# Turning the feed-forward's token-major up tiles by DMA instead of on TensorE, in a two-layer transformer block

## The chip, the cores and the metric

One Trainium2 chip, one NeuronCore of it. The metric is the device time of one execution in microseconds, as the median of several executions. The profile and the trace are of one further execution of the same program.

## The reference, cut to what matters

Two layers, each a mixer of three attention branches followed by a feed-forward block with a short causal convolution. All tensors are fp32: 256 tokens, width 1024, feed-forward width 2816. The change touches the feed-forward only.

```python
def _conv_glu_ffn(x, w_up, conv_w, conv_b, w_down):
    u = x @ w_up                                  # [256, 1024] @ [1024, 5632]
    gate, val = u[..., :D_FF], u[..., D_FF:]
    gp = jnp.pad(gate, ((0, 0), (CONV_WIDTH - 1, 0), (0, 0)))
    conv = conv_b
    for j in range(CONV_WIDTH):
        conv = conv + gp[:, j:j + seq] * conv_w[j]
    return (jax.nn.gelu(conv, approximate=False) * val) @ w_down

for l in range(2):
    x = _layernorm(ALPHA * x + mixer(x), ln1_g[l], ln1_b[l])
    x = _layernorm(ALPHA * x + _conv_glu_ffn(x, ...), ln2_g[l], ln2_b[l])
```

## The kernel before

**Panels.** All weights come in panels of 128 partitions x 2048 columns (1 MB), in one fixed order per layer. SyncE's queue loads a panel into one of six `raw` slots as two DMAs of 512 KB; it waits, before each panel, until the panel six places earlier has been used. ScalarE copies the panel to `w_hi` (four slots, rounded, `split_hi`, L1248), VectorE forms `w_lo = raw - w_hi` (`split_lo`, L1607), and TensorE computes every product in three matmuls (high x high, high x low, low x high: L738, L739, L740). A product of one up panel is 2 x 8 x 3 = 48 matmuls of 256 columns.

**The feed-forward's up product.** There are 22 tiles `f` of 128 features, one panel each (`UP_AT + f`), holding the gate and the value columns of the tile. Tiles 3 to 21 are computed feature-major (`ffn_up`, weights stationary): the result lies in one PSUM bank, gate in the first 256 columns, value in the next 256. Tiles 0, 1, 2 are computed token-major (`up_by_token`, the activations stationary), first for the tokens 0 to 127 and then for 128 to 255, since the second half of the tokens comes out of the layer norm later. ScalarE copies each result to SBUF (`u_tok`, L1372), and TensorE turns them: `turn_up` (L1146) issues four fp32 transposes for each tile, twelve a layer, into the PSUM banks that `ffn_up` would have used. The order on TensorE is: six `up_by_token`, `turn_up(0)`, `turn_up(1)`, `ffn_up(3)`, `turn_up(2)`, `ffn_up(4)` to `ffn_up(21)`, then the down product.

**What follows each tile.** A chain between ScalarE and VectorE takes the tiles in the order 0, 1, 2, ... 21: `conv_first` (ScalarE, L1380), `conv_rest` (VectorE, two operations, L1868 and L1871), `gelu` (ScalarE, L1387), `hidden` (VectorE, L1879), `hidden_hi` (ScalarE, L1391), `hidden_lo` (VectorE, L1883). Each engine runs its instructions strictly in the order written. In the loop's step for tile `f`, ScalarE does `split_hi(f + 2)` (from f = 3 on), `gelu(f - 1)`, `hidden_hi(f - 2)`, `conv_first(f)`; VectorE does `split_lo(f + 2)`, `hidden(f - 1)`, `hidden_lo(f - 2)`, `conv_rest(f)`. So a panel's split stands behind the `conv_first` of the step before. The four PSUM banks of `B_UP` are handed back by `hidden`.

**The other users of the means of the change.** In attention, ten of the twelve pairs of probability tiles are already turned by DMA: GpSimd splits the fp32 words into two planes of 16 bits (`split_probs`, L2119), SyncE's queue issues a DMA transpose of each (L698), and VectorE and GpSimd join the planes again (L1766, L2125). Ahead of the `values` products TensorE does one transpose of the identity (L1200, L1202). GpSimd has nothing to do in the feed-forward. The tensors of the two phases lie over one another in SBUF.

Of the kernel before, what the change touches and what calls it, by code (L numbers as in the profile page):

```python
# [76 lines left out]
UP_BY_TOKEN = 3  # L77

# [59 lines left out]
    residual_product=4, variances_ready=2 * NT, deviations_ready=2 * NT, up_tokens_product=UP_BY_TOKEN, up_tokens_ready=NT * UP_BY_TOKEN, up_turned=UP_BY_TOKEN,  # L138
# [4 lines left out]
def build_program(nc, x, positions, w_in, b_gate, b_forget, q_norm, kv_norm, w_uq, w_ukv, w_branch, w_out,  # L143
                  ln1_g, ln1_b, w_up, conv_w, conv_b, w_down, ln2_g, ln2_b, out):
    ctx = ExitStack()
    with ctx:
# [87 lines left out]
        s_up_turned = sem("up_turned")  # L234
# [176 lines left out]
        with ExitStack() as ffn:  # L411
            sf = sized(ffn)
            sf("beside_hidden", [P, PADS[4]])
            ht_hi = sf("ht_hi", [P, FT, T], F32R)
            ht_lo = sf("ht_lo", [P, FT, T], F32R)
# [180 lines left out]
        def halves(l, p):  # L596
# [48 lines left out]
            if p < DOWN_AT:  # L645
                return up_halves(l, s, p - UP_AT)
# [12 lines left out]
        def up_halves(l, s, f):  # L659
# [75 lines left out]
        def _(pe):  # L735
# [404 lines left out]

            def turn_up(l, f):

                pe.wait_ge(s_up_tokens_ready, at("up_tokens_ready", l, UP_BY_TOKEN + f + 1))
                for i in range(2):
                    for t in range(NT):
                        ins = pe.transpose(ps[:, B_UP[f % len(B_UP)], T * i + P * t:T * i + P * t + P],  # L1146
                                           u_tok[:, t, f, P * i:P * i + P], ident[:])
                ins.then_inc(s_up_turned, 1)

            pe.wait_ge(s_const, N_CONST)  # L1150
            for l in range(DEPTH):
# [64 lines left out]
                turn_up(l, 0)  # L1216
                turn_up(l, 1)
                ffn_up(l, 3)
                turn_up(l, 2)
                for f in range(4, FT):  # L1220
                    ffn_up(l, f)
                ng = len(DOWN_K)
                for c in range(2):
                    for g in range(ng if c == 0 else ng - SKEWED):
                        k0, nk = sum(DOWN_K[:g]), DOWN_K[g]
                        if c == 0:

                            pe.wait_ge(s_hidden_lo_ready, at("hidden_lo_ready", l, k0 + nk))
# [10 lines left out]
        def _(act):  # L1239
# [134 lines left out]
            def conv_first(l, f, buf):  # L1374

                if f < UP_BY_TOKEN:
                    act.wait_ge(s_up_turned, at("up_turned", l, f + 1))
                else:
                    act.wait_ge(s_panel_used, at("panel_used", l, UP_AT + f + 1))
                act.activation(cv[:, buf, :], ps[:, B_UP[f % len(B_UP)], 0:T], ACT.Copy,  # L1380
                                   scale=column(vec_t, V_CW + 2 * FT, f)).then_inc(s_conv_first_tap, 1)

            def gelu(l, f, buf, first):
                act.wait_ge(s_conv_ready, at("conv_ready", l, f + 1))
                if not first:
                    act.wait_ge(s_hidden_ready, at("hidden_ready", l, f - 1))
                act.activation(ge[:, buf, :], cv[:, buf, :], ACT.Gelu, bias=column(vec_t, V_CB, f)).then_inc(s_gelu_ready, 1)  # L1387

            def hidden_hi(l, f, buf):
                act.wait_ge(s_hidden_ready, at("hidden_ready", l, f + 1))  # L1390
                act.activation(tile_at(ht_hi, f), hf[:, buf, :], ACT.Copy).then_inc(s_hidden_hi_ready, 1)  # L1391
# [30 lines left out]
            for l in range(DEPTH):  # L1422
# [175 lines left out]
        def _(dve):  # L1598
# [266 lines left out]
            def conv_rest(l, f, buf):  # L1865

                dve.wait_ge(s_conv_first_tap, at("conv_first_tap", l, f + 1))
                dve.scalar_tensor_tensor(cv[:, buf, 1:T], ps[:, B_UP[f % len(B_UP)], 0:T - 1], column(vec_t, V_CW + FT, f),  # L1868
                                         cv[:, buf, 1:T], ALU.mult, ALU.add)
                dve.drain()  # L1870
                dve.scalar_tensor_tensor(cv[:, buf, 2:T], ps[:, B_UP[f % len(B_UP)], 0:T - 2], column(vec_t, V_CW, f),  # L1871
                                             cv[:, buf, 2:T], ALU.mult, ALU.add).then_inc(s_conv_ready, 1)

            def hidden(l, f, buf, first):
                dve.wait_ge(s_gelu_ready, at("gelu_ready", l, f + 1))
                if not first:

                    dve.wait_ge(s_hidden_hi_ready, at("hidden_hi_ready", l, f - 1))
                dve.tensor_tensor(hf[:, buf, :], ge[:, buf, :], ps[:, B_UP[f % len(B_UP)], T:2 * T], ALU.mult).then_inc(s_hidden_ready, 1)  # L1879

            def hidden_lo(l, f, buf):
                dve.wait_ge(s_hidden_hi_ready, at("hidden_hi_ready", l, f + 1))
# [11 lines left out]
            for l in range(DEPTH):  # L1894
# [147 lines left out]
                for f in range(FT):  # L2042
                    if f >= 3:
                        split_lo(*later(l, UP_AT + f, 2))
                    if f >= 1:
                        hidden(l, f - 1, (f - 1) % 2, f < 3)
                    if f >= 2:
# [151 lines left out]
```

## Time and profile before

| | us |
|---|---|
| median of 3 executions (lowest to highest) | 825.98 (825.44 to 826.12) |
| the profiled execution, its own time | 826.03 |
| span of the profile | 824.3 |
| TensorE matmul, busy | 812.5 (99%) |
| VectorE, busy | 596.5 (72%) |
| ScalarE, busy | 469.6 (57%) |
| GpSimd, busy | 177.3 (22%) |
| mean granted TensorE clock, share of full speed | 0.997 |

The span is the time from the first to the last instruction of the one core; the execution's own time is 1.7 us more. A matmul's record in the trace covers its whole passage, so that records overlap: the pace of a stream of matmuls is read from the distance between their starts and not from their length.

### The profile page before, as it was taken

The page shows a single profiled execution, that of the slowest core. Times are in us where ns is not written, and L with a number is a line of the kernel's source. Part 1 is how long each engine was busy: PE and PEld are TensorE (multiplying, and loading weights), DVE is VectorE, ACT ScalarE, POOL GpSimd, SP SyncE. Part 2 cuts the span into 40 slices and gives each one's busy share as a digit, 9 for nine tenths or more (in the row PEclk, how much of TensorE's full clock was granted, in tenths as well). Part 3 has the DMA queues.
Part 4 walks back from the last instruction along what each step waited for, and adds up shares of the span by engine and source line. Part 5 has one row for each costly group of instructions (what it writes and reads, how often), then busy time and mean ns, then how long its engine had stood idle before and what let it go on. Part 6 is the DMA issues. An engine that isn't in the chain of part 4 may idle for free.

```text
span 824.3 us, 15624 instructions
## 1 busy us (share of the span) xinstructions
PE 812.5 (99%) x6215; PEld 759.0 (92%) x6215; DVE 596.5 (72%) x1012; ACT 469.6 (57%) x729; POOL 177.3 (22%) x193
## 2 busy tenths in 40 slices
PE   8999999999999999999999999999999999999996
PEld 7899999899899999988889999999998999999885
DVE  5675789878886777765676568998887587777555
ACT  5675876763446555543447578767544475555440
POOL 1502944439200000000000057333660000000000
PEclk9999999999999999999999999999999999999998
DMA  9959657767578776475846694778767776664731
GB/s 305 241 141 258 209 143 204 199 161 247 171 187 215 203 202 189 151 236 181 264 122 172 117 339 148 180 186 205 212 196 209 181 200 186 187 184 155 254 116 51
DMA packets 222266, 158.86 MB, mean 193 GB/s; under 512 B 64652, under 2 KB 196336, under 8 KB 221936
## 3 DMA queue, kind: packets, MB, share of 16 engines
q1 hardware_dynamic: 213120, 150.95, 65.2%
q10 hardware_dynamic: 9072, 6.90, 3.0%
q8 instruction: 49, 0.80, 0.4%
q14 instruction: 25, 0.20, 0.1%
HBM read 148.63 MB, written 1.06 MB: 182 GB/s over the span
## 4 chain that ended last, share of the span: by engine, by line
PE 95%; DVE 1%; SPq 1%; DMA 1%; ACT 1%; ACTq 1%; issue 0%; DVEq 0%
PE ps L738 29%; PE ps L740 29%; PE ps L739 29%; PE ps L1042 3%; PE ps L1080 2%; DMA raw<-w_in 1%; PE ps L817 1%; ACTq L1300 1%; DVE w_lo L1607 1%; ACT w_hi L1248 0%; PE ps L1004 0%; PE ps L1057 0%; PE ps L1146 0%; SPq L687 0%; DVE x_tok L1858 0%
## 5 line engine op out<-in xcount | busy, mean ns | idle before, releaser
L1607 DVE TENSOR_TENSOR w_lo<-raw,w_hi 128x2048 fp32r<-128x2048 f32 (+2 forms) x140 | 304.8, 2178 | 109.7 <-ACT w_hi L1248 109.5
L738 PE MATMUL ps<-xt_hi,w_hi 128*128 128x256 f32 x1232 | 346.0, 281 | 0.0
L739 PE MATMUL ps<-xt_lo,w_hi 128*128 128x256 f32 x1232 | 341.0, 277 | 0.0
L740 PE MATMUL ps<-xt_hi,w_lo 128*128 128x256 f32 x1232 | 341.0, 277 | 0.0
L1248 ACT ACTIVATE w_hi<-raw 128x2048 fp32r<-128x2048 f32 (+3 forms) x142 | 253.1, 1786 | 90.7 <-PE ps L740 67.9
L738 PEld LDWEIGHTS ps<-xt_hi,w_hi 128*128 128x128 f32 x1232 | 231.5, 188 | 5.8 <-issue 4.7
L739 PEld LDWEIGHTS ps<-xt_lo,w_hi 128*128 128x128 f32 x1232 | 231.5, 188 | 0.2
L740 PEld LDWEIGHTS ps<-xt_hi,w_lo 128*128 128x128 f32 x1232 | 231.5, 188 | 0.0
L738 PE MATMUL ps<-w_hi,ht_hi 128*128 128x512 f32 (+1 forms) x179 | 69.1, 386 | 0.0
L740 PE MATMUL ps<-w_hi,ht_lo 128*128 128x512 f32 (+1 forms) x179 | 69.0, 386 | 0.0
L739 PE MATMUL ps<-w_lo,ht_hi 128*128 128x512 f32 (+1 forms) x179 | 69.0, 386 | 0.0
L1380 ACT ACTIVATE cv<-ps,vec_t 128x256 f32<-128x256 f32 x44 | 20.8, 474 | 81.4 <-PE ps L740 77.8
L2148 POOL COPY km_t<-km_t 32x1792 f32<-32x1792 f32 x2 | 3.4, 1675 | 295.5 <-ACT km_t L1328 295.5
L1335 ACT ACTIVATE prob<-prob,least 128x128 f32<-128x128 f32 x96 | 42.5, 445 | 22.0 <-DVE least L1743 22.0
L738 PE MATMUL ps<-w_hi,xt_hi 128*128 128x256 f32 (+2 forms) x144 | 46.2, 321 | 0.6 <-DVE w_lo L1607 0.5
L740 PE MATMUL ps<-w_hi,xt_lo 128*128 128x256 f32 (+2 forms) x144 | 45.1, 313 | 0.0
L739 PE MATMUL ps<-w_lo,xt_hi 128*128 128x256 f32 (+2 forms) x144 | 45.0, 312 | 0.0
L1868 DVE SCALAR_TENSOR_TENSOR cv<-ps,vec_t,cv 128x255 f32<-128x255 f32 x44 | 21.3, 483 | 30.2 <-ACT cv L1380 29.9
L2179 POOL TENSOR_TENSOR merged<-merged,gated 128x256 f32<-128x256 f32 x32 | 40.2, 1287 | 5.3 <-DVE gated L1791 5.2
L740 PEld LDWEIGHTS ps<-w_hi,ht_lo 128*128 128x128 f32 x179 | 33.6, 188 | 6.7
L738 PEld LDWEIGHTS ps<-w_hi,ht_hi 128*128 128x128 f32 x179 | 33.6, 188 | 6.7
L739 PEld LDWEIGHTS ps<-w_lo,ht_hi 128*128 128x128 f32 x179 | 33.6, 188 | 6.7
(268 smaller groups left out, 1304.8 us busy)
## 6 DMA issues: line engine op xcount, KB each, us to landing
raw<-ffn_w_up SPq DMA_DIRECT2D x88, 512.0 KB, 5.2
raw<-w_in SPq DMA_DIRECT2D x84, 512.0 KB, 5.8
raw<-ffn_w_down SPq DMA_DIRECT2D x32, 512.0 KB, 4.2
raw<-w_branch SPq DMA_DIRECT2D x24, 512.0 KB, 4.6
raw<-w_out SPq DMA_DIRECT2D x16, 512.0 KB, 5.6
raw<-ffn_w_down SPq DMA_DIRECT2D x24, 256.0 KB, 3.0
decay<-decay_rows ACTq DMA_DIRECT2D x2, 1024.0 KB, 8.4
ln_g<-ln_g ACTq DMA_DIRECT2D x4, 512.0 KB, 3.6
```

The lines of the kernel that those rows point to most:

```text
L738: pe.matmul(dst, a_hi, b_hi, start=first, stop=False)
L739: pe.matmul(dst, a_hi, b_lo, start=False, stop=False)
L740: return pe.matmul(dst, a_lo, b_hi, start=False, stop=last)
L817: ins = pe.transpose(ps[:, B_X[t][half], P * k:P * k + P], x_tok[:, t, P * kk:P * kk + P], ident[:])
L1042: ins = pe.matmul(ps[:, B_S[a], SPAN[t]], q[:, P * t:P * t + P], k[:, 0:P * (t + 1)], start=True, stop=True)
L1080: ins = pe.matmul(dst[HD * a:HD * a + HD, P * c:T], v, turned(i)[:, a, cols], start=c == 0, stop=c == 1)
L1248: ins = act.activation(panel_hi(l, p)[0:n, cols], panel_raw(l, p)[0:n, cols], ACT.Copy)
L1335: ins = act.activation(p, p, ACT.Exp, scale=-1.0, bias=least[:, i % 2, a, t:t + 1], accum_out=rsum[:, i % 2, a, t:t + 1])
L1380: act.activation(cv[:, buf, :], ps[:, B_UP[f % len(B_UP)], 0:T], ACT.Copy, scale=column(vec_t, V_CW + 2 * FT, f)).then_inc(s_conv_first_ta ...
L1607: ins = dve.tensor_tensor(low, panel_raw(l, p)[0:n, cols], panel_hi(l, p)[0:n, cols].bitcast(F32), ALU.subtract)
L1868: dve.scalar_tensor_tensor(cv[:, buf, 1:T], ps[:, B_UP[f % len(B_UP)], 0:T - 1], column(vec_t, V_CW + FT, f), cv[:, buf, 1:T], ALU.mult, A ...
L2179: pool.tensor_tensor(merged[:, u % KD, :], merged[:, u % KD, :], gated[:, u % NGATED, :], ALU.add).then_inc(s_merged_added, 1)
```

## The change

The twelve fp32 transposes of `turn_up` leave TensorE. In their place one transpose of the identity stands behind the six `up_by_token`; its result is read by nobody. GpSimd splits `u_tok` of each half of the tokens into two 16-bit planes (`split_up`), SyncE's queue issues one DMA transpose for each half (`cross_up`, 128 x 1536 elements of 16 bits; the first stands behind the loads of up panel 6, the second behind those of up panel 8), and GpSimd joins the planes into `u_feat` in SBUF (`join_up`, four copies for each tile). The new tensors lie over tiles 10 to 21 of `ht_hi` and 16 to 21 of `ht_lo`. The chain that follows takes the tiles in the order 3, 4, 0, 5, 1, 6, 2, 7, 8, ...; for tiles 0, 1, 2 it reads `u_feat` in SBUF where it read a PSUM bank. The split of panel `f + 2` stays in the step of tile `f`, so that no split stands in the steps of tiles 0, 1, 2.

```diff
+UP_ORDER = [3, 4, 0, 5, 1, 6, 2] + list(range(7, FT))
+UP_NO = [UP_ORDER.index(f) for f in range(FT)]
...
+                u_feat = so("u_feat", [P, UP_BY_TOKEN, 2, T])
+                up_halves = so("up_halves", [P, NT, 2, UP_BY_TOKEN * 2 * P], U16)
...
+                up_crossed = so("up_crossed", [P, NT, 4 * UP_BY_TOKEN, P], U16)
...
+        def up_psum(f, i):
+
+            if f < UP_BY_TOKEN:
+                return u_feat[:, f, i, :]
+            return ps[:, B_UP[f % len(B_UP)], T * i:T * i + T]
...
+            def cross_up(l, t):
+
+                sp.wait_ge(s_up_split, at("up_split", l, t + 1))
+                sp.dma_start_transpose(up_crossed[:, t], up_halves[:, t].rearrange("p u n -> p (u n)")).then_inc(s_up_crossed[t], 16)
...
+                    if p in (UP_AT + NLO, UP_AT + UP_BY_TOKEN - 1 + NLO):
+                        cross_up(l, p > UP_AT + NLO)
...
             def ffn_up(l, f):
 
                 pe.wait_ge(s_weights_lo, at("weights_lo", l, UP_AT + f + 1))
-                if f >= len(B_UP):
-                    pe.wait_ge(s_hidden_ready, at("hidden_ready", l, f - len(B_UP) + 1))
+                if f >= UP_BY_TOKEN + len(B_UP):
+                    pe.wait_ge(s_hidden_ready, at("hidden_ready", l, UP_NO[f - len(B_UP)] + 1))
+                elif f == UP_BY_TOKEN + len(B_UP) - 1:
+                    pe.wait_ge(s_up_tokens_ready, at("up_tokens_ready", l, NT * UP_BY_TOKEN))
...
-                turn_up(l, 0)
-                turn_up(l, 1)
-                ffn_up(l, 3)
-                turn_up(l, 2)
-                for f in range(4, FT):
+                pe.transpose(ps[:, B_R[0][1], 0:P], ident[:], ident[:])
+                for f in range(UP_BY_TOKEN, FT):
                     ffn_up(l, f)
...
-                            pe.wait_ge(s_hidden_lo_ready, at("hidden_lo_ready", l, k0 + nk))
+                            pe.wait_ge(s_hidden_lo_ready, at("hidden_lo_ready", l, max(UP_NO[:k0 + nk]) + 1))
...
-                for f in range(FT):
-                    if f >= 3:
+                for n, f in enumerate(UP_ORDER):
+                    if f >= UP_BY_TOKEN:
                         split_hi(*later(l, UP_AT + f, 2))
-                    if f >= 1:
-                        gelu(l, f - 1, (f - 1) % 2, f < 3)
-                    if f >= 2:
-                        hidden_hi(l, f - 2, f % 2)
-                    conv_first(l, f, f % 2)
+                    if n >= 1:
+                        gelu(l, n - 1, (n - 1) % 2, n < 3)
+                    if n >= 2:
+                        hidden_hi(l, n - 2, n % 2)
+                    conv_first(l, n, n % 2)
...
+            def split_up(l, t):
+
+                pool.wait_ge(s_up_tokens_ready, at("up_tokens_ready", l, UP_BY_TOKEN * (t + 1)))
+                pool.tensor_copy(up_halves[:, t], u_tok[:, t, :, :].rearrange("p f n -> p (f n)").bitcast(U16).rearrange(
+                    "p (n u) -> p u n", u=2)).then_inc(s_up_split, 1)
+
+            def join_up(l, f):
+
+                if f == 0:
+                    for t in range(NT):
+                        pool.wait_ge(s_up_crossed[t], 16 * (l + 1))
+                for t in range(NT):
+                    for i in range(2):
+                        src = up_crossed[:, t].rearrange("p (u b) k -> p u b k", u=2)[:, :, 2 * f + i, :]
+                        ins = pool.tensor_copy(u_feat[:, f, i, P * t:P * t + P].bitcast(U16).rearrange("p (k u) -> p u k", u=2), src)
+                ins.then_inc(s_up_joined, 1)
...
+                for t in range(NT):
+                    split_up(l, t)
+                for f in range(UP_BY_TOKEN):
+                    join_up(l, f)
```

VectorE's loop changes as ScalarE's does. `conv_first` waits for `s_up_joined` in place of `s_up_turned` for tiles 0, 1, 2.

## Rows read from the trace of the kernel before

**Rows 1.** The page: shares of the chain that ended last, by engine.
```profile
PE 95%; DVE 1%; SPq 1%; DMA 1%; ACT 1%; ACTq 1%; issue 0%; DVEq 0%
```

**Rows 2.** Chain that ended last, in order of time, layer 0.
```profile
248.67 0.87 PE ps L1146 x8
...
255.00 0.44 PE ps L1146 x4
```

**Rows 3.** Timeline of TensorE, layer 0: start us, length, line, operation, operands.
```profile
245.79 0.28 PE L739 MATMUL ps<-w_lo,xt_hi 128*128 128x256 f32 x1
...
248.38 0.28 PE L740 MATMUL ps<-w_hi,xt_lo 128*128 128x256 f32 x1
...
249.62 0.28 PE L740 MATMUL ps<-xt_hi,w_lo 128*128 128x256 f32 x1
...
253.03 0.28 PE L740 MATMUL ps<-xt_hi,w_lo 128*128 128x256 f32 x1
```

**Rows 4.** Window, TensorE alone: stretch, length, busy (records), granted clock, DMA share, GB/s.
```profile
256.00:350.00 94.00, 94.00 (x832) 1.00 0.65 185
```

**Rows 5.** Timeline of TensorE elsewhere: a slow stream, and two starts behind a wait.
```profile
96.50 0.28 PE L739 MATMUL ps<-xt_lo,w_hi 128*128 128x256 f32 x1
...
101.92 0.28 PE L740 MATMUL ps<-xt_hi,w_lo 128*128 128x256 f32 x1
...
241.00 0.28 PE L740 MATMUL ps<-w_hi,xt_lo 128*128 128x256 f32 x1
241.33 0.39 PE L738 MATMUL ps<-w_hi,xt_hi 128*128 128x256 f32 x1
...
601.66 0.39 PE L738 MATMUL ps<-ot_hi_last,w_hi 128*128 128x256 f32 x1
...
602.01 0.28 PE L740 MATMUL ps<-ot_hi_last,w_lo 128*128 128x256 f32 x1
...
602.92 0.28 PE L739 MATMUL ps<-ot_lo_last,w_hi 128*128 128x256 f32 x1
```

**Rows 6.** Timeline of ScalarE, layer 0 (in brackets: idle before, and what ended it).
```profile
248.71 0.39 ACT L1372 ACTIVATE u_tok<-ps 128x256 f32<-128x256 f32 x1 [2.45 <-PE ps L740]
...
255.48 0.47 ACT L1380 ACTIVATE cv<-ps,vec_t 128x256 f32<-128x256 f32 x1 [1.75 <-PE ps L1146]
...
261.74 0.51 ACT L1387 ACTIVATE ge<-cv,vec_t 128x256 f32<-128x256 f32 x1 [1.10 <-DVE cv L1871]
...
262.46 0.46 ACT L1380 ACTIVATE cv<-ps,vec_t 128x256 f32<-128x256 f32 x1
...
271.83 0.48 ACT L1380 ACTIVATE cv<-ps,vec_t 128x256 f32<-128x256 f32 x1 [1.63 <-PE ps L740]
...
277.27 0.48 ACT L1380 ACTIVATE cv<-ps,vec_t 128x256 f32<-128x256 f32 x1 [2.46 <-PE ps L740]
```

**Rows 7.** Timeline of VectorE, layer 0: the second operation of `conv_rest`.
```profile
261.22 0.48 DVE L1871 SCALAR_TENSOR_TENSOR cv<-ps,vec_t,cv 128x254 f32<-128x254 f32 x1
...
272.89 0.48 DVE L1871 SCALAR_TENSOR_TENSOR cv<-ps,vec_t,cv 128x254 f32<-128x254 f32 x1
```

**Rows 8.** GpSimd's copies by shape: count, busy us, mean ns, idle before.
```profile
L2119 POOL COPY prob_halves<-prob 128x768 uint16<-128x768 uint16 x24 | 19.3, 827 | 13.9 <-PE ps L1042 6.7 <-DVE prob L1754 6.3 <-ACT prob L1349 0.8
```

**Rows 9.** DMA issues: count, KB each, median us from issue to landing.
```profile
raw<-ffn_w_up SPq DMA_DIRECT2D x88, 512.0 KB, 5.2
...
halves_crossed<-prob_halves SPq DMA_TRANSPOSE x24, 2.8
```

**Rows 10.** Window, all engines: length, busy and records, clock, DMA share, GB/s.
```profile
248.00:254.00 6.00, 6.00 (x55) 6.00 (x54) 2.84 (x7) 3.83 (x7) 0.00 (x0) 1.00 1.20 290
```

**Rows 11.** Timelines of VectorE and GpSimd, attention of layer 0.
```profile
152.09 2.29 DVE L1607 TENSOR_TENSOR w_lo<-raw,w_hi 128x2048 fp32r<-128x2048 f32 x1
154.29 1.47 DVE L1766 COPY pts_odd<-halves_crossed 128x768 uint16<-128x768 uint16 x1
...
152.99 2.31 POOL L2125 COPY pts_odd<-halves_crossed 128x768 uint16<-128x768 uint16 x1 [3.12 <-DMA halves_crossed<-prob_halves]
```

More of the change, by code:

```diff
@@ L233, in build_program @@
         s_up_tokens_ready = sem("up_tokens_ready")
-        s_up_turned = sem("up_turned")
+        s_up_split = sem("up_split")
+        s_up_joined = sem("up_joined")
+        s_up_crossed = [sem(f"up_crossed_{t}") for t in range(NT)]
         s_conv_first_tap = sem("conv_first_tap")
@@ L413, in build_program @@
             sf("beside_hidden", [P, PADS[4]])
+            with ExitStack() as over:
+                so = sized(over)
+                so("under_up", [P, FT - 12, T])
+                u_feat = so("u_feat", [P, UP_BY_TOKEN, 2, T])
+                up_halves = so("up_halves", [P, NT, 2, UP_BY_TOKEN * 2 * P], U16)
             ht_hi = sf("ht_hi", [P, FT, T], F32R)
+            with ExitStack() as over:
+                so = sized(over)
+                so("under_crossed", [P, FT - 6, T])
+                up_crossed = so("up_crossed", [P, NT, 4 * UP_BY_TOKEN, P], U16)
             ht_lo = sf("ht_lo", [P, FT, T], F32R)
@@ L645, in halves @@
             if p < DOWN_AT:
-                return up_halves(l, s, p - UP_AT)
+                return up_columns(l, s, p - UP_AT)
             c, g = divmod(p - DOWN_AT, len(DOWN_K))
@@ L657, in first_panel, with up_columns @@
             return pieces
-        def up_halves(l, s, f):
+        def up_psum(f, i):
+            if f < UP_BY_TOKEN:
+                return u_feat[:, f, i, :]
+            return ps[:, B_UP[f % len(B_UP)], T * i:T * i + T]
+        def up_columns(l, s, f):
             return [(view(s, KD, 2 * P)[:, :, P * i:P * i + P],
@@ L1139, in up_by_token @@
                     turn_x(l, 1, 1, (1,))
[L1141 to L1148, printed above, removed]
             pe.wait_ge(s_const, N_CONST)
@@ L1863, in norm, with conv_rest, hidden, hidden_lo @@
                         ins.then_inc(s_x_ready_1, 1)
-            def conv_rest(l, f, buf):
-                dve.wait_ge(s_conv_first_tap, at("conv_first_tap", l, f + 1))
-                dve.scalar_tensor_tensor(cv[:, buf, 1:T], ps[:, B_UP[f % len(B_UP)], 0:T - 1], column(vec_t, V_CW + FT, f),
+            def conv_rest(l, n, buf):
+                f = UP_ORDER[n]
+                dve.wait_ge(s_conv_first_tap, at("conv_first_tap", l, n + 1))
+                dve.scalar_tensor_tensor(cv[:, buf, 1:T], up_psum(f, 0)[:, 0:T - 1], column(vec_t, V_CW + FT, f),
                                          cv[:, buf, 1:T], ALU.mult, ALU.add)
                 dve.drain()
-                dve.scalar_tensor_tensor(cv[:, buf, 2:T], ps[:, B_UP[f % len(B_UP)], 0:T - 2], column(vec_t, V_CW, f),
+                dve.scalar_tensor_tensor(cv[:, buf, 2:T], up_psum(f, 0)[:, 0:T - 2], column(vec_t, V_CW, f),
                                              cv[:, buf, 2:T], ALU.mult, ALU.add).then_inc(s_conv_ready, 1)
-            def hidden(l, f, buf, first):
-                dve.wait_ge(s_gelu_ready, at("gelu_ready", l, f + 1))
+            def hidden(l, n, buf, first):
+                dve.wait_ge(s_gelu_ready, at("gelu_ready", l, n + 1))
                 if not first:
[L1878 to L1882, printed above, removed]
+                    dve.wait_ge(s_hidden_hi_ready, at("hidden_hi_ready", l, n - 1))
+                dve.tensor_tensor(hf[:, buf, :], ge[:, buf, :], up_psum(UP_ORDER[n], 1), ALU.mult).then_inc(s_hidden_ready, 1)
+            def hidden_lo(l, n, buf):
+                f = UP_ORDER[n]
+                dve.wait_ge(s_hidden_hi_ready, at("hidden_hi_ready", l, n + 1))
                 dve.tensor_tensor(tile_at(ht_lo, f), hf[:, buf, :], tile_at(ht_hi, f).bitcast(F32),
@@ L2041, in _ @@
                 split_lo(l, UP_AT + 4)
-                for f in range(FT):
-                    if f >= 3:
+                for n, f in enumerate(UP_ORDER):
+                    if f >= UP_BY_TOKEN:
                         split_lo(*later(l, UP_AT + f, 2))
-                    if f >= 1:
-                        hidden(l, f - 1, (f - 1) % 2, f < 3)
-                    if f >= 2:
-                        hidden_lo(l, f - 2, f % 2)
-                    conv_rest(l, f, f % 2)
+                    if n >= 1:
+                        hidden(l, n - 1, (n - 1) % 2, n < 3)
+                    if n >= 2:
+                        hidden_lo(l, n - 2, n % 2)
+                    conv_rest(l, n, n % 2)
                 for p in range(DOWN_AT, NP):
```

23 lines of the change are left out of this document (12 added, 11 removed).

## The prediction

> **What bounds the kernel now.** I read first the shares of the chain that ended last: 95% of it is TensorE [rows 1]. Whatever leaves TensorE without starting a wait comes off the end almost whole, and what moves to GpSimd, ScalarE, VectorE or DMA costs only where TensorE comes to wait for it. Second, the chain in order of time around the change: the twelve transposes stand on it as pieces of 0.87 and 0.44 us [rows 2]. Third, TensorE's timeline on both sides of them, where the distance of starts is to be seen. The 23 rows up to 248.38 are 2.59 us apart, 0.1177 a matmul; the 31 rows from 249.62 on take 3.41 us, 0.1137, and the window over the rest of the up product has 832 records in 94.00 us, 0.113 [rows 3, 4]. The granted clock is 1.00 in both windows [rows 4, 10], so the clock is not the cause. A stream of 256-column matmuls has two paces, about 4.5 ns apart, and keeps the one it has until something interrupts it. Fourth, the timelines of ScalarE and VectorE, for how late the split of a panel may be.
>
> **What is removed.** Eight and four transposes, 0.87 + 0.44 = 1.31 us a layer on the chain, 0.109 each [rows 2]. **What is added on TensorE:** one such transpose, 0.11 us. It reads only the identity and writes a free bank, so that it waits for nothing. Net 1.20 us a layer, 2.40 us in both. Layer 1 has the same twelve.
>
> The Trainium skill (TensorE: Matmul & The Clock Gate, Part 4: PE-mode transpose) gives about 275 ns for a 128x128 transpose in a kernel, which by an estimate of mine would make the net removal 11 x 0.275 = 3.0 us a layer. The trace speaks against it: transposes overlap here and cost 0.109 each on the chain [rows 2], so the sum stays with that.
>
> **The pace behind the single transpose.** The stream before it is slow (0.1177), the 19 panels behind it are 19 x 48 = 912 matmuls. At the slow pace they cost 912 x 0.0045 = 4.1 us more a layer. No row shows one fp32 transpose directly between two such streams. The nearest are groups of two to eight that follow a running stream without a wait; I went through ten in the timeline (L1146, L1021, L1013, L817), and the stream is fast behind all ten. Against it: behind six transposes L1057, which follow score matmuls, the stream goes on slowly, 46 steps in 5.42 us, 0.1178 [rows 5]. I take fast, at 0.92; the other end is +4.1 us a layer. A gain by the pace is excluded: the stretch is fast already [rows 4].
>
> **When tiles 0, 1, 2 are ready.** Times as in layer 0. The last `u_tok` is written by 248.71 + 0.39 = 249.1 [rows 6]. GpSimd splits 768 elements in 0.83 us [rows 8]; 1536 take at most twice that, so the second half is split at 250.8. The first half of the tokens is there earlier and is split meanwhile. The transposes: half that size lands 2.8 us after its issue [rows 9], so 4 to 6 us if nothing were ahead. But between 248 and 254 the DMA engines are saturated, at 290 GB/s [rows 10], and panel 8's two loads go out at 248.6 and land in 5.2 us or more [rows 9]. Each new transpose moves 0.39 MB, 1.4 us at that rate, and the first stands before these loads. So the second lands between 250.8 + 4 = 254.8 and 248.6 + 5.2 + 3 x 1.4 + 2 = 260; I take 257.5. GpSimd joins with four copies a tile, 256 elements each: at least 0.28 us pro rata [rows 8], with a fixed part 0.5, so 2 us a tile. Tile 0 is joined at about 260, up to 262.
>
> **When they are needed.** TensorE begins panel 3 at 248.6 instead of 249.3 and takes 5.44 us a panel (271.83 to 277.27, one panel apart) [rows 6], so panel 4 ends at 259.6. ScalarE takes tile 4 up at 259.8; VectorE's second operation ends 1.54 us later (272.89 + 0.48 - 271.83) [rows 6, 7], and the next `conv_first` starts 0.76 us after that (262.46 - 261.70) [rows 6, 7], at 262.1. There tile 0 is wanted. Margin about 2 us; tiles 1 and 2 are wanted 7 and 14 us later. SyncE's queue loses nothing: while it waits for the split it would wait for panel 3 to be used (254.1) anyway. Cost of the crossing itself: nothing at my value, cover gone at 262.1.
>
> **The order of the tiles.** This is the dangerous part. Before, tiles 0 and 1 were worked off while TensorE was in panel 3; now seven panels' time (3 to 9) has to hold ten tiles. A step with a split takes 6.22 us from one `conv_first` to the end of the next `conv_rest` (255.48 to 261.70) [rows 6, 7], as ScalarE's split stands behind the first and VectorE's split behind that. Then 0.76, and the next `conv_first`. A pair (tile with a split, tile without) takes 6.98 us against a panel's 5.44: the chain slips 1.54 us each panel. From `conv_first` of tile 4 at 259.8: tile 0 at 262.1, tile 1 at 269.1, tile 2 at 276.1. Behind it stands the split of panel 9: ScalarE from 276.4 to 278.3, VectorE to 280.7 (1.91 + 2.29 with hand-overs). TensorE wants panel 9 at 248.7 + 6 x 5.44 = 281.3, its first weights 0.1 earlier. So 0.5 us is left. Behind tile 2 every panel has one tile again and the chain catches up by about 1.6 us each. Cost: 0, if nothing delays the chain by 0.5 us in its 21 us.
>
> **GpSimd beside VectorE.** Something does. GpSimd's copy at 152.99 took 2.31 us: to the end of a VectorE split (152.09 + 2.29 = 154.38) and 0.92 more. VectorE's copy at 154.29 then ended at 155.76, 0.46 behind GpSimd's end at 155.30 [rows 11]. They run one after the other. That is also what the Trainium skill says (SBUF — State Buffer, Who interferes with whom): a VectorE instruction with two SBUF inputs and a GpSimd instruction that reads SBUF exclude each other. By that rule it is the splits, `hidden_lo` and the new reads of `u_feat` that are hit, not `conv_rest` from PSUM, and the trace agrees for the split. The twelve joins run from about 259 to 268, in the chain's time; each can hold a VectorE step by up to 0.5 us. One or two will meet the chain: 0 to 1 us. Against 0.5 us of slack that is a wait of 0 to 0.5 us at panel 9; I take 0.1 a layer.
>
> **Sum:** -2.40 + 0.2 = -2.2 us, on the profiled 826.03 and, as that lies 0.05 us from the median of 825.98, on the median: 823.8. A change of 0.2% (1.65 us) is about what a measurement of this kernel can tell from none.
>
> **Rivals.**
> 1. *The wait flips the pace.* If TensorE does wait at panel 9, the stream starts anew, and 13 x 48 = 624 matmuls behind it may run slowly: +2.8 us a layer. For it: after the wait at 241.00 the pace fell from fast to the 0.1177 of rows 3 [rows 3, 5]. Against it: after the waited start at 601.66 the stream was fast again, 8 steps in 0.91 us [rows 5]. That one has the weights stationary, as `ffn_up` has. It decides if the joins and the order together delay the chain by over 0.5 us. Both layers: 823.8 + 5.6 = 829.4, slower; one layer: 826.6. Chances 0.16 and 0.12.
> 2. *The single transpose leaves the stream slow:* one layer 827.9, both 832. Chance 0.08.
> 3. *The crossing is late:* past 262.1 each microsecond of tile 0 goes into the chain, and past the slack into TensorE. Landing at 259 to 261: a wait of 0.5 to 1.5 us a layer, 824.5 to 826.5, no measurable change. For it: the saturated DMA [rows 10]. Against: the margin of 2 us. Chance 0.12.
> 4. *No gain because the end is set elsewhere.* Against it 95% of the chain [rows 1]; only as part of rival 3.
>
> **How the numbers follow.** The forecast has 0.52, with 823.2 to 824.3 of its own (no wait at all: 823.6; trace-to-trace scatter of 0.3). Faster by over 0.2%: 0.52. Same: rival 3 (0.12) and one layer flipped (0.12), less 0.02 for a late crossing that flips the pace too: 0.22. Slower: both layers flipped (0.16), the slow transpose (0.08) and that 0.02: 0.26. The range, 823.1 to 828.6, leaves out the doubly flipped cases and little below.
>
> **What would show it.** Right: no L1146; one identity transpose of 0.11 us on the chain; the step between L738 to L740 at 0.113 in the windows of both layers; the join of tile 0 before 262 and the `conv_first` of tile 1 near 269; the split of panel 9 ending near 281, with TensorE idle for at most 0.3 us. Wrong: 0.118 behind the transpose or behind panel 9; GpSimd's joins waiting for splits and tile 0's `conv_first` ended by GpSimd; TensorE idle at panels 7 to 9.

## The result, and the profile after

| | kernel before | changed kernel |
|---|---|---|
| median, us (lowest to highest, executions) | 826.06 (825.44 to 826.99, 22) | 827.96 (823.79 to 832.73, 22) |
| the profiled execution, its own time | 826.03 | 827.47 |
| span of the profile | 824.3 | 825.7 |
| GpSimd busy | 177.3 | 196.0 |
| mean granted TensorE clock | 0.997 | 0.998 |

The ratio is 1.0032, with a 95% interval of 1.0020 to 1.0044: slower, where I forecast 823.8 and faster. The 22 times of the changed kernel are more telling than their median. Two are 823.8, four lie between 826.6 and 826.9, seven between 827.3 and 828.6, nine between 829.5 and 832.8. The kernel before keeps within 1.6 us. So the forecast time exists, but in 2 executions of 22.

The page of the changed kernel, its line of busy time and the shares of the chain that ended last [rows 1]:

```profile
PE 814.2 (99%) x6193; PEld 760.5 (92%) x6193; DVE 599.2 (73%) x1012; ACT 469.2 (57%) x729; POOL 196.0 (24%) x221
...
PE 97%; DMA 1%; DVE 1%; SPq 1%; ACT 0%; issue 0%; DVEq 0%
```

TensorE is busier than before (812.5 us) although twelve transposes a layer became one. Its timeline across the single transpose, first layer 0, then layer 1 [rows 3]:

```profile
245.24 0.28 PE L764 MATMUL ps<-w_hi,xt_hi 128*128 128x256 f32 x1
...
247.85 0.28 PE L766 MATMUL ps<-w_hi,xt_lo 128*128 128x256 f32 x1
247.96 0.27 PE L1235 MATMUL ps<-ident 128*128 128x128 f32 x1
247.99 0.36 PE L764 MATMUL ps<-xt_hi,w_hi 128*128 128x256 f32 x1
248.19 0.28 PE L765 MATMUL ps<-xt_lo,w_hi 128*128 128x256 f32 x1
...
654.54 0.28 PE L766 MATMUL ps<-w_hi,xt_lo 128*128 128x256 f32 x1
...
655.01 0.27 PE L1235 MATMUL ps<-ident 128*128 128x128 f32 x1
655.04 0.36 PE L764 MATMUL ps<-xt_hi,w_hi 128*128 128x256 f32 x1
```

The same view as windows of TensorE: a fast piece of the stream before the transpose, a slow one, then two stretches of 94 us behind it (length, busy and records, granted clock, DMA share, GB/s) [rows 4]:

```profile
242.00:247.00 5.00, 5.00 (x47) 1.00 0.63 181
649.00:654.00 5.00, 5.00 (x45) 1.00 0.69 187
...
254.50:348.50 94.00, 94.00 (x800) 1.00 0.71 193
661.00:755.00 94.00, 94.00 (x832) 1.00 0.71 195
```

In layer 0 the stream comes in fast (23 steps from 245.24 to 247.85, 0.1135 each) and goes on slow: 800 records in 94 us, 0.1175 each, through all 19 panels. In layer 1 it comes in slow (four steps from 654.54 to 655.01, 0.1175) and goes on fast: 832 records, 0.113. The granted clock is 1.00 in all four rows, the full one of 2.4 GHz. The transpose itself has the same record and the same steps around it in both layers: 0.03 us to the next start, then 0.20. So the transpose costs what I said, and the stream behind it doesn't simply go on at the pace ahead of it. Nor does it take the other one by rule: in experiment 4, with one transpose, the stream comes in slow in both profiled layers and goes on fast in one and slow in the other. In layer 0 the stretch is 911 x 0.0045 = 4.1 us longer; that takes the 823.8 of the forecast to 827.9, beside the 827.47 measured.

GpSimd and SyncE's queue, layer 0: the two `split_up`, the twelve `join_up`, and the issue of the transposes between the loads [rows 8, 9].

```profile
240.61 1.46 POOL L2143 COPY up_halves<-u_tok 128x1536 uint16<-128x1536 uint16 x1 [29.54 <-ACT u_tok L1388]
248.61 1.47 POOL L2143 COPY up_halves<-u_tok 128x1536 uint16<-128x1536 uint16 x1 [6.53 <-ACT u_tok L1388]
260.36 7.46 POOL L2154 COPY u_feat<-up_crossed 128x256 uint16<-128x256 uint16 x12 [10.29 <-DMA up_crossed<-up_halves]
```

```profile
243.75 3.92 SPq L711 DMA_TRANSPOSE up_crossed<-up_halves  x1
...
252.00 4.39 SPq L711 DMA_TRANSPOSE up_crossed<-up_halves  x1
```

From issue to landing (shortest, median, longest of the four transposes), from the view of that tile:

```profile
DMA to landing us min/median/max: 6.0/7.0/8.2
```

ScalarE (`conv_first` of tiles 4, 0, 1, 2) and VectorE (steps beside the joins, and the split of panel 9), layer 0 [rows 6, 7]:

```profile
259.58 0.47 ACT L1397 ACTIVATE cv<-ps,vec_t 128x256 f32<-128x256 f32 x1 [1.55 <-PE ps L766]
...
262.04 0.51 ACT L1397 ACTIVATE cv<-u_feat,vec_t 128x256 f32<-128x256 f32 x1
...
269.75 0.49 ACT L1397 ACTIVATE cv<-u_feat,vec_t 128x256 f32<-128x256 f32 x1
...
276.75 0.49 ACT L1397 ACTIVATE cv<-u_feat,vec_t 128x256 f32<-128x256 f32 x1
```

```profile
264.39 2.54 DVE L1624 TENSOR_TENSOR w_lo<-raw,w_hi 128x2048 fp32r<-128x2048 f32 x1 [0.67 <-ACT w_hi L1264]
266.86 0.63 DVE L1897 TENSOR_TENSOR hf<-ge,u_feat 128x256 f32<-128x256 f32 x1
267.41 0.63 DVE L1902 TENSOR_TENSOR ht_lo<-hf,ht_hi 128x256 fp32r<-128x256 f32 x1
...
279.09 2.29 DVE L1624 TENSOR_TENSOR w_lo<-raw,w_hi 128x2048 fp32r<-128x2048 f32 x1 [0.77 <-ACT w_hi L1264]
```

The second transpose lands at 260.3, 2.8 us later than I took it, and tile 0 is still there when its `conv_first` comes at 262.04: the fourth of its copies ends at 262.00. Tile 1 is taken up at 269.75 (forecast 269.1), tile 2 at 276.75 (276.1), and the split of panel 9 ends at 279.09 + 2.29 = 281.38 (280.7). The 0.65 us are the joins' (below).

In this slow layer TensorE wants panel 9 only at 281.99. Layer 1 is the fast one, and there it wants it earlier against the start of panel 3. VectorE's split of panel 9 and TensorE around its first matmul of panel 9, layer 1:

```profile
685.21 2.29 DVE L1624 TENSOR_TENSOR w_lo<-raw,w_hi 128x2048 fp32r<-128x2048 f32 x1 [0.77 <-ACT w_hi L1264]
```

```profile
687.66 0.28 PE L766 MATMUL ps<-xt_hi,w_lo 128*128 128x256 f32 x1
687.78 0.28 PE L764 MATMUL ps<-xt_hi,w_hi 128*128 128x256 f32 x1
```

The split ends at 687.50 and panel 9 starts at 687.78, a plain step behind the matmul before it: no wait in this layer either.

### The profile page after: what moved, and what is told of

The parts are those of the page before. It is cut to its first block, busy times and chain, and to the rows that moved or that the text cites. A ratio compares the mean times of both kernels' runs of the same rounds, so it can differ in the third digit from the quotient of the medians.

```text
span 825.7 us, 15610 instructions
## 1 busy us (share of the span) xinstructions
PE 814.2 (99%) x6193; PEld 760.5 (92%) x6193; DVE 599.2 (73%) x1012; ACT 469.2 (57%) x729; POOL 196.0 (24%) x221
## 4 chain that ended last, share of the span: by engine, by line
PE 97%; DMA 1%; DVE 1%; SPq 1%; ACT 0%; issue 0%; DVEq 0%
PE ps L764 30%; PE ps L766 29%; PE ps L765 29%; PE ps L1068 3%; PE ps L1106 2%; DMA raw<-w_in 1%; PE ps L843 1%; PE ps L1030 0%; PE ps L1083 0%; DVE w_lo L1624 0%; ACT w_hi L1264 0%; SPq L706 0%; DVE x_tok L1875 0%; PE ps L1039 0%; PE ps L970 0%
## 5 line engine op out<-in xcount | busy, mean ns | idle before, releaser
L1624 DVE TENSOR_TENSOR w_lo<-raw,w_hi 128x2048 fp32r<-128x2048 f32 (+2 forms) x140 | 307.9, 2200 | 111.0 <-ACT w_hi L1264 110.9
L1397 ACT ACTIVATE cv<-ps,vec_t 128x256 f32<-128x256 f32 x38 | 17.9, 471 | 70.9 <-PE ps L766 70.8
L1886 DVE SCALAR_TENSOR_TENSOR cv<-ps,vec_t,cv 128x255 f32<-128x255 f32 x38 | 18.3, 481 | 25.2 <-ACT cv L1397 25.2
```

The costliest lines, as they stand in the source:

```text
L1397: act.activation(cv[:, buf, :], up_psum(f, 0), ACT.Copy, scale=column(vec_t, V_CW + 2 * FT, f)).then_inc(s_conv_first_tap, 1)
L1624: ins = dve.tensor_tensor(low, panel_raw(l, p)[0:n, cols], panel_hi(l, p)[0:n, cols].bitcast(F32), ALU.subtract)
L1886: dve.scalar_tensor_tensor(cv[:, buf, 1:T], up_psum(f, 0)[:, 0:T - 1], column(vec_t, V_CW + FT, f), cv[:, buf, 1:T], ALU.mult, ALU.add)
```

## The experiments

Times are medians with the lowest and highest; each ratio is against the kernel before, timed beside it on the same chip. The ratios follow the means: where the times fall into groups, they differ from the ratio of the medians. A break is whatever interrupts the stream of matmuls: transposes, a wait, the change from the token-major to the feature-major product. "Fast" and "slow" are the two paces, 0.1133 and 0.1178 us a matmul.

**1. How many transposes at the one place.** The changed kernel with 0, 2, 4 and 8 transposes of the identity where it has one.

```diff
-                pe.transpose(ps[:, B_R[0][1], 0:P], ident[:], ident[:])
+                for _ in range(n):
+                    pe.transpose(ps[:, B_R[0][1], 0:P], ident[:], ident[:])
```

None. 

> The changed kernel without its one transpose of the identity. Theory A (the pace of the 912 matmuls of a layer's up product is settled at the break in front of them, and one transpose settles it either way): without a break each layer goes on at whatever pace the token-major stream ends with; that was fast in layer 0 and slow in layer 1 of the profiled execution, so each layer costs 0 or 4.1 us and the times fall near 823.5, 827.6 or 831.7. Theory B (the tile order makes TensorE wait at panels 7 to 9, and the wait sets the pace): the pace changes behind those panels, not at the start, and the time is that of the changed kernel, 827.9.

Two. 

> The changed kernel with two transposes of the identity in the place of one. Theory A: a longer break settles the pace more surely; if two are enough, both layers run at 0.1133 us a matmul and the median is 823.8 + 2 x 0.11 = 824.0; if not, times are spread over 824.0, 828.1 and 832.2. Theory B: 828.1, with waits at panels 7 to 9.

Four. 

> The changed kernel with four transposes of the identity. Theory A: as with the four of the kernel before ahead of its panel 4, the pace is fast in both layers of every run; median 823.8 + 6 x 0.11 = 824.5. Theory B: 828.6.

Eight. 

> The changed kernel with eight transposes of the identity, as many as the kernel before had there. Theory A: fast in both layers of every run; 823.8 + 14 x 0.11 = 825.3, under the kernel before by 0.7. Theory B: 829.5.

| transposes | us (executions) | ratio, interval | profiled execution: layer 0, layer 1 |
|---|---|---|---|
| 0 | 826.65, 824.11 to 831.81 (12) | 1.0009, 0.9994 to 1.0024 | fast then slow from panel 9; fast |
| 2 | 831.88, 823.96 to 833.46 (12) | 1.0055, 1.0035 to 1.0076 | slow; slow |
| 4 | 828.39, 824.53 to 832.96 (12) | 1.0029, 1.0013 to 1.0046 | slow; fast |
| 8 | 829.27, 828.49 to 833.68 (6) | 1.0054, 1.0035 to 1.0073 | fast; slow |

My theory that a longer break brings the fast pace back each time fell: two, four and eight are no better than one (1.0032). Nor is the single transpose to blame as such. With nothing between the two streams the stretch starts fast in both profiled layers, yet in layer 0 something else goes wrong at panel 9. TensorE's timeline there without the transpose, layer 0 and then layer 1:

```profile
280.53 0.28 PE L765 MATMUL ps<-xt_lo,w_hi 128*128 128x256 f32 x1
280.64 0.28 PE L766 MATMUL ps<-xt_hi,w_lo 128*128 128x256 f32 x1
280.93 0.39 PE L764 MATMUL ps<-xt_hi,w_hi 128*128 128x256 f32 x1
281.15 0.28 PE L765 MATMUL ps<-xt_lo,w_hi 128*128 128x256 f32 x1
...
686.63 0.28 PE L766 MATMUL ps<-xt_hi,w_lo 128*128 128x256 f32 x1
686.75 0.28 PE L764 MATMUL ps<-xt_hi,w_hi 128*128 128x256 f32 x1
```

VectorE's split of panel 9 in layer 0 is `278.58 2.29`; it ends at 280.87, and TensorE, which wanted the panel at 280.75, starts at 280.93. In layer 1 it is `684.30 2.29` and ends at 686.59, in time. Windows of 22 us of TensorE ahead of and behind panel 9, layer 0 and then layer 1:

```profile
256.00:278.00 22.00, 22.00 (x196) 1.00 0.98 231
283.00:305.00 22.00, 22.00 (x189) 1.00 0.67 185
661.00:683.00 22.00, 22.00 (x196) 1.00 0.95 230
690.00:712.00 22.00, 22.00 (x196) 1.00 0.72 196
```

A wait of 0.18 us (0.29 between two starts, for 0.11) stands in layer 0 alone. It has 196 records before it and 189 after it: the pace fell. Layer 1 has no such wait, and 196 and 196. This is my first rival: one wait, and one fall of the pace right behind it.

**2. The old twelve transposes put back as ballast.** In the changed kernel, at their old places and in their old banks; nobody reads their output, and the tiles still go by DMA. `turn_up` is the one of the kernel before.

```diff
+            def turn_up(l, f):
...
-                pe.transpose(ps[:, B_R[0][1], 0:P], ident[:], ident[:])
-                for f in range(UP_BY_TOKEN, FT):
+                turn_up(l, 0)
+                turn_up(l, 1)
+                ffn_up(l, 3)
+                turn_up(l, 2)
+                for f in range(4, FT):
                     ffn_up(l, f)
```

> The changed kernel, but TensorE again does the twelve transposes of u_tok at their old places and into their old banks, with their results unread (the DMA route still feeds the tiles), and no transpose of the identity. Theory C (what keeps the kernel before at the fast pace is the kind and place of its transposes: u_tok as operand, banks 6, 7 and 4, one group in the midst): 826.0 as before, fast in both layers of all runs. Theory D (the pace is drawn anew at any break, and what differs is the rest: DMA and GpSimd traffic, tile order, the wait at panel 9): slow layers in part of the runs, the median 827 to 831.

826.34 us (825.33 to 829.83, 11 executions), ratio 1.0004 (0.9993 to 1.0014); fast in both profiled layers. TensorE does the old work, and all that the change moved to GpSimd, SyncE's queue and the DMA runs beside it: it costs nothing that can be measured. What was lost is the pace. Four of the eleven times are still above 826.9, one of them 829.83; the kernel before, timed beside it, reached 828.12 too.

**3. A group ahead of each of panels 5 to 21, in the kernel before.** One transpose of the identity (n = 1), four, and four of tile 2 of `u_tok` in the place of the identity.

```diff
                 for f in range(4, FT):
+                    if f > 4:
+                        for _ in range(n):
+                            pe.transpose(ps[:, B_R[0][1], 0:P], ident[:], ident[:])
                     ffn_up(l, f)
```

> The kernel before with one transpose of the identity (into bank 3) ahead of each of panels 5 to 21, so that the pace may change 17 times in a layer. If one transpose redraws the pace: a mixture of fast and slow panels, and each transpose shows how likely. If the fast pace survives a break: all fast. Cost of the transposes 34 x 0.11 = 3.7 us, 829.8 if all fast, up to 837 if all slow.

> The same with four transposes of the identity at each of these places: 34 x 0.44 = 15.0 us, 841 if all fast. Draws as before; if four make the fast pace surer than one, the share of fast panels rises.

> The same with four transposes of u_tok of tile 2, as the kernel before has ahead of its panel 4, into bank 3. If the operand matters (theory C), nearly all panels are fast, 841, where the identity gave a mixture; if not, the same mixture.

They took 837.72, 841.60 and 843.81 us (two executions each; ratios 1.0135, 1.0182, 1.0209). The pace of each panel matters more. Windows of 4.5 us inside panels 4 to 11 with one transpose ahead of each from panel 5 on:

```profile
257.20:261.70 4.50, 4.50 (x43) 1.00 0.84 229
262.40:266.90 4.50, 4.50 (x41) 1.00 0.85 233
268.10:272.60 4.50, 4.50 (x40) 1.00 0.80 229
274.30:278.80 4.50, 4.50 (x42) 1.00 0.82 233
279.50:284.00 4.50, 4.50 (x41) 1.00 0.84 236
285.20:289.70 4.50, 4.50 (x40) 1.00 0.84 232
291.00:295.50 4.50, 4.50 (x41) 1.00 0.82 232
297.20:301.70 4.50, 4.50 (x43) 1.00 0.84 237
```

4.5 us hold 1.5 steps more at the fast pace than at the slow one; panels 4, 7 and 11 have 42 or 43 records, the others 40 or 41. From start to start the 17 panels from panel 5 on go slow, slow, fast, then three slow and one fast in turn, the same in both layers. With four transposes of the identity all 34 panels are fast; with four of `u_tok` three panels of four. **Within one execution the paces behind the breaks are not independent draws: they follow an order that repeats every four panels.** Something must pass from one break to the next, or advance with the program, that the pace itself doesn't show; the runs don't tell which of the two.

The stretch is also not the only place where the pace varies. The two stretches of the trace with one transpose are 9.6 us longer than in the kernel before, its span 11.8 us; the other 2.2 us lie in parts where the two kernels are the same. That is also why its time passed the 837 that I had given for the case that all panels are slow. So a single time tells how many slow layers there were only roughly.

**4. The order of the tiles.** `UP_ORDER` with tiles 1 and 2 set further back, so that ScalarE and VectorE can catch up between two tiles without a split; with one transpose, with none, and with the twelve old ones as ballast.

```diff
-UP_ORDER = [3, 4, 0, 5, 1, 6, 2] + list(range(7, FT))
+UP_ORDER = [3, 4, 0, 5, 6, 1, 7, 8, 2] + list(range(9, FT))
```

> The changed kernel with the tiles taken up in the order 3, 4, 0, 5, 6, 1, 7, 8, 2 instead of 3, 4, 0, 5, 1, 6, 2, so that the chain of ScalarE and VectorE can catch up between tiles 0, 1 and 2; the single transpose stays. Theory (the pace behind a single transpose depends on how the stream enters it, and the wait at panel 9 is a second cause of its own that comes from the order of the tiles): no idle step at panel 9; the times fall in three groups only, 823.8, 827.9 and 832, and none near 826.6; the median stays above that of the kernel before, at 827 to 829. Rival (the order alone makes the stretch slow): the median falls to 824 and the paces are fast in both layers.

> The same spread order, and without the single transpose of the identity. Theory (two causes, both now taken away: nothing between the two streams, and no wait at panel 9): the stretch is fast from its start to panel 21 in both layers, 911 steps of 0.1133 us, the times lie close together at 823.4 to 824.2, and it is faster than both kernels, ratio 0.997. Rival (the wait at panel 9 isn't made by the order of the tiles, or what flips the pace there isn't the wait): times between 824 and 832 as without the transpose in the old order, median 826 to 827.

> The changed kernel with the twelve old transposes of u_tok at their old places between the products (their output is read by nobody) and no transpose of the identity, in the spread order. Theory (the old pattern, eight transposes, 48 products, four transposes, brings the stream to the fast pace each time, and what scattered above 826.5 in the unspread order was the wait at panel 9): times within 825.2 to 826.6, all steps fast in both layers, ratio to the kernel before 0.999 to 1.001. Rival (the scatter has to do with the crossing or GpSimd, not with the order): some times between 827.5 and 830 again.

| | us (executions) | ratio, interval | above 826.5 us |
|---|---|---|---|
| one transpose | 827.52, 823.57 to 832.82 (12) | 1.0032, 1.0011 to 1.0053 | 10 of 12 |
| none | 823.68, 822.57 to 831.59 (12) | 0.9985, 0.9966 to 1.0005 | 3 of 12 |
| old twelve | 825.95, 825.35 to 826.38 (11) | 0.9998, 0.9990 to 1.0007 | 0 of 11 |

VectorE's timeline with one transpose and the new order: the split of panel 9 ends at 277.74, 2.9 us before TensorE starts the panel at 280.61.

```profile
275.45 2.29 DVE L1624 TENSOR_TENSOR w_lo<-raw,w_hi 128x2048 fp32r<-128x2048 f32 x1 [0.77 <-ACT w_hi L1264]
```

The split is far from late now, and with one transpose the median is as bad as before: the order is not the main cause. My expectation that no time would lie near 826.6 was missed by one, the profiled 826.81; its windows have 831 and 801 records in 94 us, one layer fast, one slow, and no wait. So a time near 826.7 alone doesn't prove a wait. Without a transpose nine of the twelve times lie between 822.5 and 824.0, with the lowest of all runs among them, but the profiled execution is the worst of them:

```profile
254.50:348.50 94.00, 94.00 (x801) 1.00 0.71 193
661.00:755.00 94.00, 94.00 (x801) 1.00 0.70 194
```

Its stream came in slow and stayed slow in both layers, where in experiment 1 a slow one turned fast at the same place. "Fast from the start in both layers" fell too. With the old twelve all eleven times lie between 825.35 and 826.38, as expected, where four of eleven were above 826.9 in experiment 2; that speaks for a small share of the order, from two comparisons on different chips.

**5. What of the old pattern settles the pace.** No transpose behind the six `up_by_token` but `n3` ahead of panel 3 and `n4` ahead of panel 4, all of the identity, in the order of experiment 4.

```diff
-                pe.transpose(ps[:, B_R[0][1], 0:P], ident[:], ident[:])
                 for f in range(UP_BY_TOKEN, FT):
+                    for _ in range({3: n3, 4: n4}.get(f, 0)):
+                        pe.transpose(ps[:, B_R[0][1], 0:P], ident[:], ident[:])
                     ffn_up(l, f)
```

> The changed kernel in the spread order (3, 4, 0, 5, 6, 1, 7, 8, 2), with eight transposes of the identity ahead of panel 3 and four ahead of panel 4: the old kernel's counts and places, but one operand and one bank of PSUM. Theory (it is the places and counts of the breaks that lead to the fast pace each time): times close together, 825.3 to 826.4, fast in both layers behind the second group. Rival (it is the operands or banks of the old transposes): some times 4 or 8 us above that, as with eight ahead of panel 3 alone.

> The same with four ahead of panel 3 and four ahead of panel 4. Theory (a second group a panel behind the first settles the pace, as groups of four ahead of every panel did in 34 panels of 34): fast behind panel 4 in both layers each time, times close together at 824.5 to 825.6, ratio 0.999. Rival (it needs just eight ahead of panel 3, or luck): groups of times near 825, 829 and 833.

> The same with none ahead of panel 3 and four ahead of panel 4. If one group of four, a panel behind the change of operands, is enough, the times lie together at 823.8 to 824.8 and it is the fastest of the kernels that are so each time; if two breaks are needed, as theory says, groups near 824, 828 and 832.

> The same with two ahead of panel 3 and two ahead of panel 4. If any two breaks settle the pace, the times lie together at 823.8 to 824.8; if the number within a group counts (one transpose a panel gave three slow panels of four, four a panel gave none), groups near 824, 828 and 832.

> One transpose of the identity ahead of panel 3 and one ahead of panel 4, spread order. If any second break a panel later settles the pace: times together at 823.6 to 824.4. If the number within a group counts (single transposes ahead of every panel left three panels of four slow): groups near 824, 828 and 832.

| n3, n4 | us (executions) | ratio, interval | above 826.9 us |
|---|---|---|---|
| 8, 4 | 825.82, 825.22 to 826.68 (11) | 0.9998, 0.9989 to 1.0006 | 0 of 11 |
| 4, 4 | 825.49, 824.86 to 825.78 (11) | 0.9994, 0.9986 to 1.0003 | 0 of 11 |
| 2, 2 | 824.57, 824.03 to 824.99 (11) | 0.9983, 0.9974 to 0.9991 | 0 of 11 |
| 0, 4 | 824.55, 824.12 to 832.83 (12) | 1.0005, 0.9986 to 1.0024 | 5 of 12 |
| 1, 1 | 827.99, 823.83 to 832.31 (12) | 1.0012, 0.9992 to 1.0031 | 8 of 12 |

Two groups of two or more, a panel apart, keep the time at its lower end in all 33 executions; one group of four ahead of panel 4, or two single transposes, don't. In the profiled execution with 2 and 2 panel 3 is slow and what follows panel 4's group is fast, in both layers. TensorE's windows, first in panel 3, then behind the second group, layer 0 and layer 1:

```profile
249.00:254.00 5.00, 5.00 (x45) 1.00 1.05 286
256.00:350.00 94.00, 94.00 (x832) 1.00 0.71 195
653.00:658.00 5.00, 5.00 (x45) 1.00 1.16 295
661.00:755.00 94.00, 94.00 (x832) 1.00 0.68 194
```

In the five profiled executions with two such groups (those of experiment 6 among them) panel 3 is slow in six of ten layers, and what follows the second group is fast in all ten.

The operands and banks of the old transposes are not needed for the steady time, their places are: 8 and 4 of the identity are as steady as the old twelve. That the operand has no effect at all is not shown; in experiment 3 `u_tok` and the identity gave different orders.

**6. The better version again, and its order.** 2 and 2 in the order of experiment 4 (`spread`) and in that of the change (`near`), side by side.

> The changed kernel in its own order (3, 4, 0, 5, 1, 6, 2), with two transposes of the identity ahead of panel 3 and two ahead of panel 4. Theory (the order leaves TensorE waiting at panel 9 in part of the executions, and such a wait lets the pace fall): as in the spread order for the fastest, 824.0 to 825.0, with a part of the times at 826.5 to 830, which the spread order in the same call doesn't have. Rival (with the pace settled by two groups the order makes no difference): both at 824.0 to 825.0.

> The kernel with two and two in the spread order again, beside the other two of this call. Theory and rival alike: 824.0 to 825.0, all times together, ratio to the kernel before 0.998 with the whole interval under 1.

Near: 824.72 (824.00 to 827.85, 11 executions), ratio 0.9983 (0.9974 to 0.9991). Spread: 824.53 (824.10 to 825.92, 11), 0.9980 (0.9971 to 0.9988). One time above 826.5 against none: with the pace settled the order is worth at most little, and these runs don't separate it from nothing. No profiled layer of the two waits at panel 9, so what made the one time of 827.85 is not known. **The version with 2 and 2 in the spread order beats both kernels**: in two comparisons it is 0.17% and 0.20% faster than the kernel before, and 827.96 - 824.5 = 3.5 us below the changed kernel's median.

## Why the prediction was wrong

**The step that failed** is "the pace behind the single transpose", which I took "fast, at 0.92", with the slow case as a rival at 0.08. Ten groups in the trace of before were fast behind them, and I read them as ten draws. They were not: in experiment 3 the paces repeat every four panels, alike in both layers, so that the rows of one trace are no independent draws, and the 22 executions of the changed kernel scatter over 9 us. Behind the single transpose the profiled execution went slow in layer 0, 107.4 us from the first start to the last, and fast in layer 1, 103.3 us. The kernel before is steady by its own shape, eight transposes, a panel, four; 8 and 4, 4 and 4, and 2 and 2 are so too, one group alone isn't. The change took away both groups and put one transpose in their place. The row that spoke against me, the six transposes behind which the stream went on slowly [rows 5], should have weighed more.

**The size of that case** was right: I priced one slow layer at 827.9 and two at 832; the times stand near 827.4 to 828.5 and up to 832.7, and the one layer profiled as slow is 4.0 us longer than the fast one.

**What was removed and added**: right. The two lowest times of the changed kernel, 823.79 and 823.80, are those forecast for two fast layers, 823.8 (823.6 without a wait); neither was profiled, so that both layers were fast in them is read from the time. The 0.109 of a transpose on the chain [rows 2] was of the right size: from 2, 2 to 8, 4 there are 16 more in two layers and 1.25 us between the medians, 0.08 each; from 2, 2 to 4, 4 there are 8 more and 0.92 us, 0.12 each.

**The crossing**: mis-sized, without effect. I took the landing at 257.5 with 260 as the upper end; it was 260.3. Half the size lands 2.8 us after its issue [rows 9], this one 6.0 to 8.2 us, and issuing it holds SyncE's queue for 3.9 to 4.4 us (half the size: 1.2 us in the median), which I had not counted. Tile 0 was still in time: its `conv_first` at 262.04 has no idle time before it. But of the margin of 2 us 0.04 was left in layer 0, and 0.6 in layer 1. The Trainium skill (DMA: Bandwidth & Descriptors, Latency and other measured facts) gives DMA transposes an effective 261 GB/s in the slower of its two cases, by an estimate from which 0.39 MB would take 1.5 us; with 6.0 us or more from issue to landing here, the measurement decides.

**The order of the tiles**: right in mechanism, 0.65 us late. The slack of 0.5 us is used up by "GpSimd beside VectorE": the split beside the joins took 2.54 for 2.29, `hidden` 0.63 for 0.42, `hidden_lo` 0.63 for 0.42, in sum 0.67. That is the exclusion of [rows 11]; the Trainium skill (SBUF — State Buffer, Who interferes with whom) says it, and the trace agrees. That would exceed the slack by 0.15, but layer 0 was slow and wanted the panel later. In layer 1, the fast one, the joins delayed the chain by 0.3 to 0.4 us and no wait came. Over all profiled executions with this order of the tiles, nine layers came up to panel 9 at the fast pace: in one TensorE waited, 0.18 us (experiment 1), in the others the split ended 0.16 to 0.6 us before panel 9 started. So the wait is possible, as I said, and rarer than the 0.1 us a layer that I put into the sum for it.

**Rival 1, the wait flips the pace**: seen once, in experiment 1. Layer 0 had the wait and fell to the slow pace right behind it; it took 106.3 us from the first start to the last, against 103.3 in layer 1, for 13 x 48 x 0.0045 = 2.8 us forecast. No other profiled layer waits at panel 9, so how often such a wait does this is open. If it is a second cause beside the first, it is the smaller: the order that leaves no wait leaves the median at 827.5.

**The shown and the open.** Shown: the loss is the pace of the stream behind the break, at a granted clock of 1.00, and not GpSimd, DMA or the chain (experiment 2); it depends on where and how many breaks stand there (3, 5), and the paces of one execution are tied to each other (3). Open: what ties them, whether it is carried by the stream at all, and why it differs between executions of one program. One start on TensorE ahead of the stretch differs from trace to trace, the one at 241 us that waits for `xt_lo`: it stands 0.27 behind the start ahead of it in the changed kernel, 0.33 in the kernel before [rows 5]. That this start decides the pace was my guess, and the traces speak against it as the only cause. Without the transpose it stands 0.28 behind in layer 0 in either order of the tiles, and the stretch begins fast in one and slow in the other; with 1 and 1 it stands 0.33 behind in both layers (`241.30` to `241.62`, `644.51` to `644.84`), and the stretch is fast in layer 0 and slow from panel 4 on in layer 1. No kernel without this wait was tried.

## What to carry to other kernels

A stretch of 900 matmuls whose pace can be 4% lower outweighs twelve transposes: before taking work out ahead of such a stretch, run it some ten times and look at the spread, and read the distance of starts in windows, not the busy time. Many alike rows of one trace can be little more than one observation when they hang on one course of events. Two groups of two or more cheap transposes of the identity, a panel apart, kept the time at its lower end here in 54 of 55 executions, for 0.1 us a transpose; why they do is not known.

## What the runs showed of the hardware that I had not expected

- A stream of 256-column matmuls at a granted clock of 1.00 has two paces, 0.1133 and 0.1178 us, and kept one through up to 912 matmuls. With one transpose of the identity between panels the fast pace came every fourth panel; with four it came each time.
- A DMA transpose within SBUF of 128 x 1536 elements of 16 bits held its issuing queue for 3.9 to 4.4 us and landed after 6.0 to 8.2 us, against 1.2 and 2.8 us (medians) for half the size.
- GpSimd's copy of 1536 elements (1.46 us) held a VectorE split that began 0.3 us after it: `240.91 3.30` in place of 2.29.
